# Recurrent heads: VectorE's "turned matrix" step is joined to the step behind it, and other threads' steps run after both

## The reference, cut to what matters

```
a_kk = jnp.where(strict, jnp.einsum('bhnic,bhnjc->bhnij', kb, kc) * gam, 0.0)
sol = lax.linalg.triangular_solve(a_kk + eye, rhs, left_side=True, lower=True, unit_diagonal=True)
u, w = sol[..., :dv], sol[..., dv:]
a_qk = jnp.einsum('bhnic,bhnjc->bhnij', qc, kc) * gam
def step(state, inp):
    v_new = un - jnp.einsum('bhck,bhkv->bhcv', wn, state)
    o = (jnp.einsum('bhck,bhkv->bhcv', qn * jnp.exp(gn)[..., None], state)
         + jnp.einsum('bhij,bhjv->bhiv', aqk, v_new))
    ...
```

## Time and profile before

| | |
|---|---|
| median of 3 runs | 3259.35 us (3258.98 to 3262.5) |
| the profiled execution's own time | 3257.08 us |
| its span in the profile | 3255.2 us |
| busy share: PE, VectorE, ScalarE, GpSimd | 95%, 47%, 33%, 11% |
| mean granted clock of PE | 0.978 of full speed |

### The profile page before, as it was taken

The page is one execution under the profiler, slowest core; times in us unless marked ns, Lnnn a source line. Parts: engine busy times, 40 slices in busy tenths (PEclk is TensorE's granted clock), DMA queues, the critical chain, the costliest instruction groups (busy, mean ns, idle before and its releaser), DMA issues.

```text
span 3255.2 us, 39275 instructions
## 1 busy us (share of the span) xinstructions
PE 3094.8 (95%) x16399; PEld 2579.9 (79%) x16399; DVE 1540.7 (47%) x2165; ACT 1065.2 (33%) x2300; POOL 363.1 (11%) x433
## 2 busy tenths in 40 slices
PE   7999999999999999999999999999999999997998
PEld 4788888877777877887877888888888877777887
DVE  4455556566653224131255344444444658532453
ACT  3443443444443213232320241111122333213453
POOL 0122222232231000000010000000000111001111
PEclk9999999999999999999999999999999999997999
DMA  2211111011111111111353221111111310111001
GB/s 108 66 49 49 40 53 46 33 40 33 33 40 59 46 55 49 43 43 49 117 205 123 107 76 59 52 48 43 52 51 40 123 68 27 65 39 46 27 27 40
DMA packets 59362, 192.78 MB, mean 59 GB/s; under 512 B 7697, under 2 KB 15377, under 8 KB 49970
## 3 DMA queue, kind: packets, MB, share of 16 engines
q1 hardware_dynamic: 58320, 189.19, 16.7%
q10 hardware_dynamic: 866, 1.09, 0.1%
HBM read 156.28 MB, written 33.98 MB: 58 GB/s over the span
## 4 chain that ended last, share of the span: by engine, by line
PE 83%; DVE 10%; ACT 4%; issue 2%; POOL 0%; DMA 0%; ACTq 0%; DVEq 0%; POOLq 0%
PE ps L2389 20%; PE ps L2391 20%; PE ps L2390 20%; PE ps L2266 3%; PE ps L702 3%; PE ps L708 3%; PE ps L1701 2%; PE ps L3226 1%; DVE ar L1109 1%; PE ps L739 1%; PE ps L745 1%; PE ps L3285 1%; PE ps L754 1%; PE ps L1666 1%; PE ps L753 1%
## 5 line engine op out<-in xcount | busy, mean ns | idle before, releaser
L2389 PE MATMUL ps<-r,r 128*128 128x512 f32 (+4 forms) x2848 | 1134.0, 398 | 42.4 <-DVE r L230 12.2
L2391 PE MATMUL ps<-r,r 128*128 128x512 f32 (+4 forms) x2848 | 1071.8, 376 | 0.0
L2390 PE MATMUL ps<-r,r 128*128 128x512 f32 (+4 forms) x2848 | 1069.5, 376 | 0.0
L2389 PEld LDWEIGHTS ps<-r,r 128*128 128x128 f32 (+2 forms) x2848 | 544.0, 191 | 140.4 <-issue 24.4
L2391 PEld LDWEIGHTS ps<-r,r 128*128 128x128 f32 (+2 forms) x2848 | 541.0, 190 | 101.0
L2390 PEld LDWEIGHTS ps<-r,r 128*128 128x128 f32 (+2 forms) x2848 | 544.3, 191 | 82.3 <-issue 5.7
L2389 PE MATMUL ps<-r 128*128 128x512 f32 x512 | 199.7, 390 | 0.8 <-DVE r L2382 0.8
L2391 PE MATMUL ps<-r 128*128 128x512 f32 x512 | 199.3, 389 | 0.0
L2390 PE MATMUL ps<-r 128*128 128x512 f32 x512 | 199.2, 389 | 0.0
L2639 DVE TENSOR_TENSOR ar<-ar,ps 128x512 f32<-128x512 f32 x224 | 151.2, 685 | 92.5 <-PE ps L2391 92.1
L2377 ACT ACTIVATE r<-ar 128x2048 fp32r<-128x2048 f32 x48 | 91.7, 1910 | 260.8 <-PE ps L2391 254.4
(11 more groups left out here) (323 smaller groups left out, 4152.0 us busy)
## 6 DMA issues: line engine op xcount, KB each, us to landing
ar<-wst SPq DMA_DIRECT2D x72, 1024.0 KB, 4.8
ar<-wst SPq DMA_DIRECT2D x56, 512.0 KB, 4.0
ar<-x SPq DMA_DIRECT2D x16, 512.0 KB, 10.5
ar<-sc_g SPq DMA_DIRECT2D x32, 256.0 KB, 4.7
sc_h<-ar SPq DMA_DIRECT2D x32, 256.0 KB, 2.2
sc_x<-ar SPq DMA_DIRECT2D x16, 512.0 KB, 2.8
ar<-sc_x SPq DMA_DIRECT2D x16, 512.0 KB, 4.4
sc_b<-ar SPq DMA_DIRECT2D x24, 260.0 KB, 2.0
```

The source lines that it names most:

```text
L2389: t.do.matmul(o, l[0], r[0], start=first, stop=False)
L2390: t.do.matmul(o, l[0], r[1], start=False, stop=False)
L2391: return t.do.matmul(o, l[1], r[0], start=False, stop=last)
```

## The change

One `yield` moves. Before, MT was one step and the two masked copies with the decay products were the next; now all are one step, and the two steps behind it are empty. The thread keeps its number of steps.

```
@@ dve_inv
             v.do.scalar_tensor_tensor(out=four(MT), in0=KQ[:, :, 0, :], scalar=-1.0, in1=four(MT), op0=ALU.mult, op1=ALU.mult).then_inc(*inv_dve.tick(k("MT")))
-            yield
             v.wait_ge(dve_const, "masks")
...
                 o = v.do.tensor_tensor(four(aqs[kept(h, part)][d]), KQ[:, :, 1, :], four(Eg[d]), ALU.mult)
             o.then_inc(*inv_dve.tick(k("aq")))
+            yield
             yield
             for n in LV:
```

## The result

| | before | now |
|---|---|---|
| median (4 runs each, same chip) | 3259.16 us (3258.85 to 3262.5) | 3278.12 us (3275.75 to 3280.35) |
| profiled execution, its span | 3257.08, 3255.2 us | 3279.78, 3277.7 us |
| mean granted clock of PE | 0.978 | 0.975 |

A forecast was written before the change was run, and what follows sets the result against it. PE bounds the kernel, through its work and its waits. 10.3 + 5.4 + 7.5 + 0.5 - 3.0 + 3.2 = 23.9 us slower than 3257.1, plus 2.3 for the median: 3283 us, range 3269 to 3296.

The forecast's parts named there:

- L739 behind the joined step: Even stages: L739 waits for the scan's later L1226; +10.3 us in stages 2, 4, 6, +5.4 in 8 to 14.
- L739's delay is not on the path: Rival, even stages: PE reaches L739 late enough, so only the gain at L702 is left; 3247 us, chance 0.04.
- the covers that the sum takes off: Even stages: L702's earlier waits, 0.26 us in stage 2 and 1.92 in stage 12, offset L739's delay.
- The detour over the tanh: Stages 3, 5, 7: late L1109 delays tanh, squares, L998 and so L708; +7.5 us taken, 3.9 to 9.8.
- the discount for L1209: Stages 3, 5, 7: a shorter L1209 gives part back; net 2.5 us each taken instead of 3.25.
- The gain in stages 9, 11, 13: No tanh waits and L1192 comes 1.0 us earlier, shortening L702's waits; -3.0 us, range 0 to -8.4.
- Stage 1: The tanh's delay without squares, 0.9 us late less up to 0.6 of L230's wait; +0.5 us, 0.3 to 0.9.
- The clock: Behind PE's long waits: two more falls to the lower clock level, at 1.7 us each; +3.2 us.
- The rival with a fall behind each of the ten: Each of the ten new long PE waits ends in a fall of the clock; 3290 us, chance 0.24.
- Smaller loss: Rival: only the direct wait counts, shorter tanh detour, L1209 wins everywhere, clock unchanged; 3274 us, chance 0.17.
- given back: Rival: later waits for L230, L1213 or a DMA absorb the loss, so no change; chance 0.05.

The follow-up runs named there:

- The even stages alone: The joined step in the even stages alone, odd stages as in the kernel before: 3276.69 us, ratio 1.0056.
- Half the join: Against the kernel before, the yield moved between the two masked copies in all stages, so only the first joins MT: 3260.12 us, ratio 1.0006.

## Why the prediction was right, and where its sizes were off

The direction and the mechanism held: 3278 in a range of 3269 to 3296, 5 us under the forecast. Step by step:

- **L739 behind the joined step.** Forecast 3.7 us late in stage 2 and 3.3 in stage 12; measured from L1185, 3.63 and 3.22. The timeline of stage 12 of the changed kernel, to be set beside the earlier trace rows:

```profile
857.60 0.60 DVE L1226 SCALAR_TENSOR_TENSOR ar<-ps,ar 128x128 f32<-128x128 f32 x2
...
858.25 1.22 PE L739 MATMUL ps<-ar 128*128 128x128 f32 x4 [3.06 <-DVE ar L1226]
```

  What stays was over-sized a little: +9.3 for +10.3 in stages 2, 4, 6, and +4.5 for +5.4 in 8 to 14. In stage 2 the 3.63 us at L739 are 3.22 at L702, with the 0.26 that is covered, and 3.11 at L708, so the delay shrinks by 0.26 more within PE's own queue. The even stages alone gave the whole loss, so the rival "L739's delay is not on the path" falls. Half the join tested the covers that the sum takes off, 0.3 us and 1.92 of L702's wait: of its delay of 1.25 us, 0.7 are left in stages 2, 4, 6, and of 0.83 nothing in 8 to 14.
- **The detour over the tanh.** Forecast L708 3.25 us late and about 4 us of idle ScalarE; measured 3.14 and 4.17. Here the term was mis-sized, +9.9 for the +7.5 taken, at the upper end of 9.8. The step that failed is the discount for L1209: it is indeed short now (1.31 us, not under 1), but L230 is held in its place, in all three stages. The Trainium skill, "SBUF — State Buffer", section "SBUF: two separate sides", gave that upper end: a VectorE instruction with two SBUF inputs and a GpSimd instruction that reads SBUF exclude each other for a whole instruction. The trace agrees, since L1339 gets its turn between L1209 and L230 and the second of them pays.
- **The gain in stages 9, 11, 13.** Forecast -3.0; measured -7.1 without the clock. This is the term that was furthest off. The step that failed is how often and how far L1209 would be short: 1.5 was taken in two stages and nothing in the third, of a bound of 2.8 each. L1192 came earlier by 1.0 as worked out, and in all three stages L1209 began ahead of L1339 and was short, which brought 1.4 more. The trace of before hides this in stage 11, where a fall of the clock had already made L1209 short.
- **Stage 1.** Forecast +0.5; measured +0.74.
- **The clock.** Forecast +3.2, two falls more than five; measured +2.5 us in the profiled pair. Windows of the changed kernel right behind three of its long waits, in stages 4, 5 and 12, to be read as the earlier trace rows:

```profile
375.60:380.00 4.40, 4.40 (x18) 3.83 (x19) 0.00 (x0) 0.38 (x1) 0.00 (x0) 0.61 0.00 0
446.20:450.60 4.40, 3.72 (x21) 2.93 (x21) 3.32 (x3) 2.06 (x3) 4.32 (x2) 1.00 0.00 0
...
858.30:862.70 4.40, 4.40 (x18) 4.11 (x19) 1.02 (x1) 0.59 (x2) 0.00 (x0) 0.50 0.00 0
```

  Seven of the ten long waits end in a fall, that of stage 12 in one twice as long, so seven falls stand against five, as forecast. Not every one costs the 1.7 of the forecast: those behind L708 in stages 3 and 7 were mostly taken in by the next wait (L2389 waits 0.76 and 0.70 us for L230 there, and 2.14 in stage 5, which has no fall), and the one that went in stage 11 had cost 0.15. The rival with a fall behind each of the ten would have given 3290 and did not come.
- **Smaller loss, or given back.** The first would have given 3274 by a short detour, L1209's turn won and no clock term. It came nearest to the gain in stages 9, 11, 13 (5.6 for 7.1); its other parts did not come. Nothing absorbed the loss later.

In the order of the sum the errors are -1.0, -0.9, +2.4, +0.2, -4.1 and -0.7, together -4.1, from 23.9 to the 19.8 of these stages. That the median came out 5 us under the forecast is partly luck: the loss by the tanh's detour was put 2.4 too small and the gain 4.1 too small, and these work against each other.

## What to carry to other kernels

Before you bring one instruction forward in a fixed order, look at what was standing between: a short instruction for another engine that is waited for within a microsecond (L1226) must not go behind four others that put it off by 3.6 us, whichever thread they are of. Follow the delay through the queues of third engines, since work that nobody needs yet (the squares ahead of L998) adds to it. And treat one `yield` in a generator as many edits, one for each kind of stage; here, without the clock, three stages gained 2.4 us each, eleven lost 0.7 to 3.3, and an edit with only the gaining ones was faster than both.

## What was not expected of the hardware

- **Falls of the clock** follow waits of about 2 us as well as those of 3.05 to 3.6. In the kernel before it was five of twelve, in the changed one seven of the ten long ones, and with the even stages joined five of seven; the same wait in stage 8 had one in one kernel and none in the other (PEclk 0.61 and 1.00). Counted over the 16 stages in all eleven traces, 14 of the 20 waits of over 3 us had one, 32 of the 69 of 1.68 to 2.17 us, and none of the 106 of 1.0 to 1.6 us. One costs about 1.6 us where PE has no slack, and about 0.15 in stages 3 and 7 of the changed kernel and 11 of the one before, where a later wait was shorter for it. The Trainium skill, "TensorE: Matmul & The Clock Gate", section "HAM oscillation", describes such bursts split by waits, each burst starting at the lower clock; a fall behind each is not seen here, and 14 of 20 against 32 of 69 is more often, but too few cases to be sure. What decides a single one stays open.
- **VectorE and GpSimd hold each other in turn.** Where L1339 arrives at two VectorE instructions back to back in stages 3, 5 and 7, one of the two is long: L1209 2.73 us and L1339 1.90 before, L230 2.85 and L1339 2.35 now, but 1.32 and 1.25 for the two when L1339 is elsewhere. Freeing the first instruction gained nothing while the second was the one that PE needed.
